# Blocks of the identity multiplied on TensorE while it waits, in a kernel of four hybrid, attention, recurrent and expert layers

## The reference

```
x = first_block(x, ...)            # 2 x hybrid_layer, rms_norm(h, final_g)
for i in range(2):                 # second block
    hl = modulate(rms_norm_2(xl, norm1_g[i]), sh1, sc1)   # and hc of the context
    oc, ol = neighbourhood_attention(...) if i == 0 else rwkv7_bidirectional(...)
    xl = xl + gt1 * ol
    hl = modulate(rms_norm_2(xl, norm2_g[i]), sh2, sc2)
    xl = xl + gt2 * expert_choice_ffn(hl, router[i], w1[i], w3[i], w2[i])
```

## Time and profile before

| | |
|---|---|
| median of 3 runs | 4213.89 us (4209.35 to 4219.35) |
| the profiled execution | 4218.45 us |
| its span, first to last instruction | 4216.3 us |
| mean granted TensorE clock | 0.926 |
| TensorE matmul busy | 3629.6 us, 86% |
| VectorE busy | 1550.6 us, 37% |
| ScalarE busy | 967.9 us, 23% |

### The profile page before, as it was taken

The page is one execution under the profiler, slowest core; times in us unless marked ns, Lnnn a source line. Parts: engine busy times, 40 slices in busy tenths (PEclk is TensorE's granted clock), DMA queues, the critical chain, the costliest instruction groups (busy, mean ns, idle before and its releaser), DMA issues. The chain is left out here.

```text
span 4216.3 us, 73041 instructions
## 1 busy us (share of the span) xinstructions
PE 3629.6 (86%) x30758; PEld 2259.0 (54%) x30758; DVE 1550.6 (37%) x3268; ACT 967.9 (23%) x1906; POOL 190.3 (5%) x225
## 2 busy tenths in 40 slices
PE   6989899896998959999985987999999995687787
PEld 5736386553446543334333445888888893322222
DVE  3646256441127431222225014444544444311111
ACT  2115111322117310000001004554444441100000
POOL 0000000000002000000000001000000000000000
PEclk9998899988999969999997997999999997799999
DMA  5751257112201128999991100000000002299998
GB/s 158 180 190 43 64 130 206 61 41 69 67 27 47 64 81 313 346 362 344 342 343 46 60 26 11 2 2 2 3 3 3 3 3 90 86 380 397 402 398 351
DMA packets 148916, 605.86 MB, mean 144 GB/s; under 512 B 19200, under 2 KB 21824, under 8 KB 131584
## 3 DMA queue, kind: packets, MB, share of 16 engines
q1 hardware_dynamic: 142272, 579.57, 38.1%
q0 software_dynamic: 6336, 21.63, 2.2%
HBM read 576.39 MB, written 31.07 MB: 144 GB/s over the span
## 5 line engine op out<-in xcount | busy, mean ns | idle before, releaser
L1704 PE MATMUL psum<-ring,big 128*64 128x512 f32 (+1 forms) x6144 | 910.2, 502 | 106.8 <-DMA ring<-moe_w 91.0
L1704 PEld LDWEIGHTS psum<-ring,big 128*64 128x64 f32 (+1 forms) x6144 | 302.3, 125 | 675.4 <-issue 475.9
L371 PE MATMUL psum<-h_uT,ring 128*128 128x264 f32 x1280 | 290.5, 387 | 0.0
L2408 ACT ACTIVATE X<-ring 64x512 f32<-64x512 f32 x336 | 211.1, 628 | 254.7 <-PE psum L2248 144.4
L371 PEld LDWEIGHTS psum<-h_uT,ring 128*128 128x128 f32 x1280 | 242.0, 190 | 46.5 <-issue 5.8
L500 DVE SCALAR_TENSOR_TENSOR h_O<-h_O,cond_silu 128x512 f32<-128x512 f32 x336 | 226.9, 746 | 100.9 <-DMA h_O<-ada_w 100.8
L1215 PE MATMUL psum<-ring,big 128*128 128x512 f32 x576 | 251.1, 596 | 2.0 <-PEq L55 2.0
L2223 PE MATMUL psum<-ring 64*64 64x64 f32 x6016 | 229.1, 221 | 9.6 <-DVE ring L2590 5.3
L2223 PEld LDWEIGHTS psum<-ring 64*64 64x64 f32 x6016 | 215.3, 135 | 17.6 <-issue 11.0
L1850 DVE TENSOR_TENSOR big<-big,psum 128x512 f32<-128x512 f32 (+1 forms) x48 | 27.3, 597 | 469.7 <-PE psum L1704 469.7
L1985 PE MATMUL psum<-big,ring 128*128 128x512 f32 (+1 forms) x464 | 170.4, 530 | 31.7 <-DVE big L1956 24.0
(11 more groups left out here) (353 smaller groups left out, 4684.7 us busy)
## 6 DMA issues: line engine op xcount, KB each, us to landing
ring<-moe_w SPq DMA_DIRECT2D x192, 2048.0 KB, 10.5
h_O<-ada_w SPq DMA_DIRECT2D x192, 256.0 KB, 2.9
ring<-w_in SPq DMA_DIRECT2D x16, 2048.0 KB, 13.2
ring<-na_w_qkv SPq DMA_DIRECT2D x6, 2048.0 KB, 7.9
ring<-w_out SPq DMA_DIRECT2D x4, 2048.0 KB, 9.1
bias_rows<-na_table SPq DMA_DIRECT2D x16, 480.0 KB, 14.5
ring<-bias_rows SPq DMA_DIRECT2D x16, 360.0 KB, 2.9
rows<-big SPq DMA_DIRECT2D x10, 512.0 KB, 4.6
```

Source lines behind the costliest of these rows:

```text
L371: last = nc.tensor.matmul(bank(k, pair_bank(q) + h, NH), w[:, a, f * P:(f + 1) * P], uT[:, a, halves[h]], start=a == 0, stop=a == KD - 1)
L1704: last = nc.tensor.matmul(bank(k, b, r.width)[q * r.n:(q + 1) * r.n, :], rowsT[:, half * HALF_K + n, r.first:r.first + r.n], w[:, n, q * r ...
L2408: last = nc.scalar.activation(to(z)[rows, :, par, :], pairs(src, z)[rows], ACT.Copy)
```

## The change

A new helper issues groups of four matmuls. Each multiplies a 64x64 block of the identity by the same block, one group takes all the four combinations of row half and column half of the array. The results go to the first 64 columns of PSUM banks 6 and 7 and are read by nobody. It is called with 28 groups at the head of TensorE's list in every `norm_turn`, with 120 groups in `second_start`, and in `route` with 28 groups behind the router's products and 80 groups behind the first transposes. Nothing is removed, and no other engine's list changes.

```diff
+def keep_busy(k, groups):
+
+    for n in range(groups):
+        for row, col in ((0, 0), (HEAD, HEAD), (0, HEAD), (HEAD, 0)):
+            k.nc.tensor.matmul(bank(k, 6 + (row != col), HEAD)[col:col + HEAD, :], k.ident[row:row + HEAD, 0:HEAD],
+                               k.ident[row:row + HEAD, 0:HEAD], start=True, stop=True)
@@ norm_turn
         @block.tensor
         def _(pe):
+            keep_busy(k, 28)
             pe.wait_ge(s.normed, len(tiles))
             turn_tensor(k, pe, s, xn, segs, strided)
@@ second_start
+        @block.tensor
+        def _(pe):
+            keep_busy(k, 120)
+
@@ route
             last.then_inc(s.logits, 1)
+            keep_busy(k, 28)
             pe.wait_ge(s.ready, 1)
             for t in range(nt):
                 last = nc.tensor.transpose(bank(k, 1, P, t * P)[0:EXPERTS, :], aff[:, t, 0:EXPERTS], k.ident[:, :])
             last.then_inc(s.turned, 1)
+            keep_busy(k, 80)
             pe.wait_ge(s.ready, 2)
```

## The result

The changed kernel takes 4242.9 us (median of 8 runs, 4232.2 to 4247.5) beside 4220.3 us for the kernel before on the same chip (8 runs, 4209.4 to 4225.8): a ratio of 1.0050, 95% interval 1.0035 to 1.0064. By the medians that is 22.6 us slower (a ratio on record is not the quotient of two medians, so the two can differ by a tenth of a per cent). The prediction had said +4.9 us, and 4208 to 4233 us. It started from a median of three, 4213.9; the eight runs here put the kernel before 6.4 us higher. With +22.6 us on the lower start the time would still lie outside, at 4236.5.

A forecast was written before the change was run, and what follows sets the result against it. The prediction took the chain through the norm, second_start and route stages, where TensorE waits, to bound the kernel. Terms of -0.4 and +5.3 us summed to +4.9 us, a median of 4218.8 us, range 4208 to 4233.

The forecast's parts named there:

- second_start: 480 matmuls in this stage take 16.6 us, hidden behind the stage's loads with 6 us to spare: 0.
- Pace of the four quadrants: Each added matmul, four quadrants working side by side, takes 31 ns at full clock and 53 ns at half clock.
- The first rival: Added matmuls: four quadrants no faster than two, 62 ns warm and 106 ns cold; +19.6 us, 4233.5 us; chance 22%.
- Norm bursts: 112 matmuls in each of six norm stages: hidden, but mostly ending too early to keep transposes warm; -0.4 us.
- The rival in which the clock survives the gap: Norms: clock holds longer behind a dense burst, all gain half their cold stretch; -6.4 us, 4207.5 us; chance 8%.
- Router bursts: 112 matmuls behind the router's products, two layers: transposes 3.2 and 3.0 us late, less 0.4 and 0.5; +5.3 us.
- The rival in which bursts do not lift the clock: All bursts run at 53 ns throughout, no transpose faster; +7.6 us, 4221.5 us; chance 8%.
- Rank bursts: 320 matmuls behind route's first transposes, two layers: 9.9 us, hidden within waits of 16.08 and 21.56 us; 0.

The follow-up runs named there:

- start_loop: The full change, but with second_start's 480 matmuls as a TensorE loop of 8 turns over 15 groups: 4250.7 us, ratio 1.0071 to the kernel before.
- shift_128: The kernel before plus 8 groups (32 matmuls, 128 instructions) in the first norm only: 4240.4 us, ratio 1.0040.
- start_loop_0: start_loop with 8 groups more in the first norm: 4234.4 us, ratio 1.0018 to the kernel before.
- shift_64: The kernel before plus 4 groups (16 matmuls, 64 instructions) in the first norm only: 4229.6 us, ratio 1.0013.
- shift_1344: The kernel before plus 21 groups (336 instructions) in each of the first four norms: 4231.1 us, ratio 1.0022.
- warm_norms_0: The kernel before plus looped bursts in the norms only, 12 groups a turn, the fourth norm 6 turns of 15: 4218.5 us, ratio 0.9993.

## Why the prediction was wrong

Two steps failed: `second_start`, priced at 0, cost 8.6 us, and code that moves, which had no term, cost 5.9 us at the jumps of the first expert layer. The other steps held in the main.

**Pace of the four quadrants: right.** Forecast 31 ns a matmul warm and 53 cold. The norm's burst in the second expert layer runs 224 records in 3.50 us: 15.6 ns a record, 31 ns a matmul. Behind that layer's router, where the clock is at 0.50, the records follow each other at 26.6 ns, 53 a matmul. The first rival (quadrants no faster than two) is refuted: in the loop of `start_loop` 480 matmuls take 15.4 us, where it needed 31.4. That rival's time for the stage, +8.6 us, is just what the changed kernel shows, and by another cause; its +19.6 us for the kernel is also nearer to the measured time than any other forecast, by luck. The pattern within the burst (packs at full pace, and pauses) tells the two apart, the total doesn't.

**Norm bursts: right in the main.** Hidden, ended too early, cold transposes. (The first took 7.7 us, with a pause of 1.9 us in it, and not 5.2.) The -0.4 us did not come: all transposes together took 42.2 us, 41.2 before. In the last norm of the changed kernel the burst ends at 3649.79, and the windows read:

```profile
3651.00:3652.00 1.00, 0.00 (x0) 0.00 (x0) 0.61 (x2) 0.29 (x2) 0.00 (x0) 1.00 0.00 0
...
3653.00:3654.00 1.00, 0.00 (x0) 0.00 (x0) 1.00 (x3) 0.00 (x0) 0.00 (x0) 0.50 0.00 0
```

Some 2.5 us, then, sooner than the 4.3 to 4.5 us on which the forecast rested. But this is not a property of the short burst. In `shift_128`, which has no burst there, the last long product ahead of this norm ends at 3646.67, and the clock falls at 3649.1, 2.4 us later:

```profile
3649.00:3650.00 1.00, 0.00 (x0) 0.00 (x0) 0.00 (x0) 1.00 (x2) 0.00 (x0) 0.56 0.92 393
```

In the changed kernel's fourth norm it held for 4.9 us behind the same burst. Two readings were too few. The rival in which the clock survives the gap is refuted: in all six norms of the changed kernel it fell before the transposes started.

**second_start, "hidden, 0": this step failed.** 16.6 us was 405 x 31 + 75 x 53 ns, the pace of TensorE alone. (Even the 75 cold ones were wrong: with the burst 1.5 us behind the last product the clock did not fall first, and the loop ran at 1.00 throughout.) Behind each 128 records the next 256 instructions have to come, every 3.5 us at best and slower beside the stage's loads, so 1920 instructions need seven packets and 30.6 us. Cost 8.6 us here, and 12.6 to 13.2 in the two kernels with this burst alone, where the lower clock added to it. `start_loop` has the same matmuls and one fetch in place of seven, and the cost is gone. The loads of the stage were later too (the last at 24.4 us from its start, against 21.9), but they were not what ended it.

**Router bursts, +5.3: right.** +3.6 and +3.5 us, less 0.6 and 0.4 for faster transposes: +6.1. (The bursts start 0.1 us before the products end, not the 0.3 us of the forecast, for which it showed no row.) The rival in which bursts do not lift the clock is refuted by those transposes.

**Rank bursts, "9.9 us, hidden": right in result, wrong in size.** 16.2 us in the second expert layer, in a wait of 16.1: only just hidden. In `start_loop_0` it ended 1.3 us too late.

**No term at all for code that moves.** This is the second step that failed: the prediction priced no code outside the bursts. The first expert layer lost 6.7 us, 5.9 of them at its three jumps back, with 5440 added instructions (a shift of 64) ahead of it. That the place does it rests on `shift_64` and `shift_1344`, which change little else and bring one long jump each, on `warm_norms_0` with all three and `start_loop_0` with one, and on the nine kernels at other shifts with none. Why it is one in some and three in others stays open. The scan was lucky: 5888 added instructions are a whole number of 256, and it took 1102.0 us as before. With a shift of 128 there, the two kernels that have one lost 12 and 21 us; TensorE's idle time in the scan grew by 13.0 and 8.5 us.

**What is left.** Of the 24.1 us between the two profiled executions, 8.6 + 5.9 + 6.1 = 20.6 are accounted for. The last router's products add 3.0 us (13.37 for 10.38), because the clock fell 3.3 us earlier in them; the first router's give back 1.2. The attention layer was 2.8 us shorter. Why the clock fell when it did, and what made the attention layer shorter, stays open.

## What to carry to other kernels

Count added instructions as well as their time: here a straight run of small matmuls got 256 instructions each 3.5 us at best, and the runs of 1280 and 1920 instructions were bound by that (those of 448 went through in some places and paused in others), while the same work in a loop of 240 instructions ran without a pause. When an edit should cost nothing and moves the time anyway, look at the jumps back of later loops and at the clock in them, and repeat the kernel with a few hidden instructions more: in this case 32 matmuls were worth 16 us either way, more than any single term of the edit itself. A burst that is to keep the clock up has to last until just before the work that should profit: one that ended 4.6 us too early brought nothing, gaps of about 2 us worked in most norms and not in all, and the whole kernel gained 6.6 us in one version and 4.0, not clear of noise, in its near twin.

## What the runs showed of the hardware

- **Supply of instructions.** A packet on queue 8 is 16 KB, 256 instructions. In quiet stretches TensorE used one in 2.10 us and got the next 3.47 us after the last; beside loads the pauses grew to 4.9 us, and once to 7.45. The Trainium skill, "Runtime: NRT & Kernel Launch", section "Instruction fetch mechanics", says that instructions are streamed in 16 KiB blocks of 256; the trace agrees. It also says that the cost of crossing a block's border is mostly hidden. For dense small matmuls this trace does not agree: 1.38 us at each border.
- **Jumps.** The same section says that a jump to a block which is not at hand stalls the engine. The trace agrees: 2.0 to 5.8 us at the jumps of the long loops of the scan and the first expert layer, nothing measurable at those of a body of 240 instructions.
- **Place.** The same loop, moved by 128 instructions, pauses twice a turn in place of once, and TensorE is idle for 13.0 us more in the scan (8.5 in the second kernel with this shift). The scans lasted 12 and 21 us longer; the rest of the 21 is time at the lower clock.
- **Clock.** Where it was read here, it fell 2.4 to 4.9 us after the last matmul, behind short bursts without a pause (2.5 and 4.9 us in the changed kernel's last and fourth norm) as behind long products (4.3 and 4.5 us, 2.4 us in `shift_128`).
- **Quadrants.** Matmuls of 64x64 in all four quadrants in turn run at 31 ns each (two records) at full clock, twice as fast as in two quadrants.
